# Two of eight weight units per chunk, not three, multiplied as plain f32 in the conv input projection

## The reference

```python
def _conv_mixer(h, w_in, b_in, dw_w, dw_b, ln_g, ln_b, w_out, b_out):
    u = h @ w_in + b_in                     # 256 x 2048 by 2048 x 4096
    a, gt = jnp.split(u, 2, axis=-1)
    u = a * jax.nn.sigmoid(gt)              # the gated product
    u = lax.conv_general_dilated(           # 31 taps, each channel by itself
        u, dw_w[:, None, :].astype(u.dtype), window_strides=(1,),
        padding=[(CONV_WIDTH - 1, 0)],
        dimension_numbers=('NWC', 'WIO', 'NWC'),
        feature_group_count=D_MODEL) + dw_b
    u = jax.nn.silu(_layer_norm(u, ln_g, ln_b))
    return u @ w_out + b_out
```

## Time and profile before

| | us |
|---|---|
| median of 3 runs | 2627.55 |
| lowest, highest | 2624.93, 2643.36 |
| the profiled execution | 2643.36 |
| its span, first to last instruction | 2641.7 |
| TensorE busy | 2566.5 (97%) |
| VectorE busy | 1866.8 (71%) |
| ScalarE busy | 1289.4 (49%) |
| GpSimd busy | 235.7 (9%) |
| `conv_in`, first to last matmul of its units | 1572.3 to 1791.0 |

### The profile page before, as it was taken

How to read it: one execution, slowest core, us unless ns; L and a number is a source line. 1 busy time by engine, 2 the same in 40 slices (tenths; PEclk the granted TensorE clock), 3 DMA queues, 4 the chain that set the end, 5 groups by cost and what they waited for, 6 DMA issues and landing times.

```text
span 2641.7 us, 38949 instructions
## 1 busy us (share of the span) xinstructions
PE 2566.5 (97%) x14482; PEld 2194.0 (83%) x14482; DVE 1866.8 (71%) x2076; ACT 1289.4 (49%) x1682; POOL 235.7 (9%) x270
## 2 busy tenths in 40 slices
PE   8999999999999999999999989998989999999999
PEld 7888888787877887888888878997878888888887
DVE  6796658778878766877678756988566555565565
ACT  5645445544434546454455456676544344343443
POOL 2000000010010000000000004873000000000000
PEclk9999999999999999999999989998989999999999
DMA  6644437898999765768877744453545665656655
GB/s 208 175 129 118 130 113 270 291 335 304 316 331 325 243 225 171 270 209 282 264 241 252 251 140 154 147 167 110 185 144 192 194 187 191 191 185 195 188 188 168
DMA packets 291488, 553.13 MB, mean 209 GB/s; under 512 B 17121, under 2 KB 96018, under 8 KB 290578
## 3 DMA queue, kind: packets, MB, share of 16 engines
q1 hardware_dynamic: 270994, 442.06, 51.6%
q0 software_dynamic: 18720, 102.77, 11.6%
q10 hardware_dynamic: 1632, 6.29, 0.7%
HBM read 548.96 MB, written 2.10 MB: 209 GB/s over the span
## 4 chain that ended last, share of the span: by engine, by line
PE 79%; DVE 7%; DMA 7%; issue 3%; ACT 3%; SPq 0%; POOLq 0%; DVEq 0%; ACTq 0%
PE sums L668 30%; PE small L668 10%; PE sums L697 9%; PE small L697 9%; PE sums L699 5%; DMA mod_raw<-in_mod_w_dram 5%; PE small L699 4%; PE sums L716 4%; DVE w_lo L622 2%; PE sums L718 2%; DVE mod_acc L1333 2%; ACT w_hi L613 1%; PE small L1696 1%; DMA raw<-in_w_br_dn_dram 1%; PE sums L1833 0%
## 5 line engine op out<-in xcount | busy, mean ns | idle before, releaser
L613 ACT ACTIVATE w_hi<-raw 128x1024 fp32r<-128x1024 f32 x814 | 860.5, 1060 | 1208.5 <-PE sums L668 344.3
L622 DVE TENSOR_TENSOR w_lo<-raw,w_hi 128x1024 fp32r<-128x1024 f32 x814 | 1004.2, 1242 | 617.4 <-ACT w_hi L613 615.2
L697 PE MATMUL sums<-x_two,w_hi 128*128 128x512 f32 x1024 | 367.3, 403 | 5.1 <-DVE x_two L977 2.8
L697 PE MATMUL small<-x_two,w_hi 128*128 128x512 f32 x1024 | 362.5, 399 | 0.0
L699 PE MATMUL sums<-x_two,w_lo 128*128 128x256 f32 x1024 | 289.6, 283 | 0.0
L699 PE MATMUL small<-x_two,w_lo 128*128 128x256 f32 x1024 | 287.6, 281 | 0.0
L668 PE MATMUL sums<-w_hi,x_two 128*128 128x512 f32 x896 | 283.3, 394 | 2.1 <-DVE w_lo L622 2.1
L668 PE MATMUL sums<-w_hi,y_hi 128*128 128x512 f32 x672 | 265.2, 395 | 12.7 <-issue 7.0
L668 PE MATMUL sums<-w_lo,y_hi 128*128 128x512 f32 x672 | 263.2, 392 | 0.0
L668 PE MATMUL sums<-w_hi,y_lo 128*128 128x512 f32 x672 | 263.1, 392 | 0.0
L1333 DVE SCALAR_TENSOR_TENSOR mod_acc<-mod_raw,cond,mod_acc 128x1536 f32<-128x1536 f32 x120 | 217.8, 1815 | 55.9 <-DMA mod_raw<-in_mod_w_dram 55.6
(11 more groups left out here) (412 smaller groups left out, 3953.5 us busy)
## 6 DMA issues: line engine op xcount, KB each, us to landing
raw<-in_mlp_w_dram SPq DMA_DIRECT2D x256, 512.0 KB, 4.3
raw<-in_w_in_dram SPq DMA_DIRECT2D x198, 512.0 KB, 4.7
mod_raw<-in_mod_w_dram POOLq DMA_DIRECT2D x128, 768.0 KB, 6.5
raw<-in_w_up_dram SPq DMA_DIRECT2D x128, 512.0 KB, 3.9
raw<-in_w_down_dram SPq DMA_DIRECT2D x64, 512.0 KB, 4.5
raw<-in_conv_w_in_dram SPq DMA_DIRECT2D x128, 256.0 KB, 3.7
raw<-in_w_o_dram SPq DMA_DIRECT2D x32, 512.0 KB, 6.5
raw<-in_conv_w_out_dram SPq DMA_DIRECT2D x32, 512.0 KB, 4.2
```

Source lines behind the costliest of these rows:

```text
L613: act.activation(w_hi[:, s.slot(k), :], raw[:, s.slot(k), :], ACT.Copy).then_inc(hi_ready, 1)
L622: dve.tensor_tensor(w_lo[:, s.slot(k), :], raw[:, s.slot(k), :], w_hi[:, s.slot(k), :].bitcast(F32), ALU.subtract).then_inc(lo_ready, 1)
L697: pe.matmul(to[:, b, :], w_hi[:, s.slot(k), c], both, start=kt == 0, stop=False, skip_group_check=True)
```

## The change

```diff
 CV_C = 8
 CV_B = KT // CV_C
-CV_WHOLE = (0, 3, 6)
+CV_WHOLE = (0, 4)
 POOL_TAPS = 13
```

## The result

The changed kernel takes 2645.48 us in the median of 7 runs (2634.10 to 2649.46), the kernel before 2627.55 us in the median of 7 (2624.93 to 2643.36). The ratio is 1.0056, 95% interval 1.0033 to 1.0079. A second comparison of the same two kernels gave 1.0029 (1.0012 to 1.0046). So the change makes the kernel a little slower, by 0.3 to 0.6%, where 0.2% (5.6 us) was forecast. Two profiled executions of the kernel before have spans of 2641.7 and 2627.9 us, two of the changed kernel 2634.4 and 2641.4 us: a single span can't show a difference of this size. The stage inside them can, because it repeats within 0.7 us.

The account below looks back on a forecast made before the run. In `conv_in` TensorE and VectorE were taken as nearly level, with VectorE setting the pace afterwards. -0.6, +0.6, +7.85 and -2.3 us gave +5.6, so 2633 us from the median of 2627.55, range 2621 to 2643.

Parts of the forecast that it names:

- TensorE's saving: `conv_in`: one whole unit fewer in 8 chunks saves 8 x 0.57 = 4.5 us; the four-pass sum of 7.7 was rejected.
- VectorE's cycle: `conv_in`: a sixth `w_lo` at 1.6 us lengthens the cycle from 25.99 to 27.8 us, against TensorE's 25.9.
- The two small adds: VectorE in `conv_in`: they fall in the first of the five cycles once and lie in the wait behind the gated product.
- The last chunk: Last cycle of `conv_in`: ScalarE's `tap_diag` are done in time, so 24.6 us becomes 22.3, a gain of 2.3.
- The first part: Start of `conv_in`: chunk 1's gated product 0.6 us earlier, then the 30.4 us to chunk 2 about 0.6 longer.
- the front's 3.1 us: Front of `conv_in`: added roundings for x and unit 3, costed at nothing under unit 0 at half clock, else 3.1 us.
- Where TensorE waits: TensorE in `conv_in`: waits for `w_lo` at units 5 to 7 from chunk 3 on, 1.9 us a chunk.
- The lock: `w_lo` waiting for a whole GpSimd add (1.84 us) would take 3.1 us, total 2642; ruled out by the longest, 2.25.
- TensorE as the bound: Rival for `conv_in`: VectorE keeps up, the 4.5 us and TensorE's 2.1 us of waits go, 2621 us; chance 0.12.
- the two cancel: Rival for `conv_in`: VectorE at its lower bound, 2628 us; chance 0.15.
- The clock rival: Rival for `conv_in`: TensorE's new waits lower its granted clock, 7.5 us in all, 2641 us; chance 0.07.
- The rival of late loads: Rival for `conv_in`: loads behind slot 0 late, wait behind the gated product 1 us longer in eight chunks, 2641; chance 0.06.

Follow-up runs that it names:

- the quiet pair: GpSimd's adds cut from 256 to 8 positions, in the changed kernel and in the kernel before; ratios 0.9978 and 0.9986 to the kernel before.
- quiet_pool: The changed kernel with GpSimd's adds cut from 256 to 8 positions; ratio 0.9978 to the kernel before.
- whole_0: The changed kernel with only unit 0 whole, all others split; ratio 1.0054 to the kernel before.
- early_hi: The changed kernel with `w_hi` of unit 5 written ahead of the products that wait for the gated product; ratio 1.0013 to the kernel before.
- early_hi_pool14: As early_hi, with one tap of chunks 0 to 6 moved from VectorE to ScalarE and GpSimd; ratio 1.0034 to the kernel before.

## Why the prediction was right

The forecast was 2633 us, +5.6; its mechanism, that VectorE's queue becomes the bound and its cycle is the sum of its instructions plus the wait behind the gated product, is what the runs show. The times lie above it: 1.0056 and 1.0029 of 2627.55 are 2642.3 and 2635.2 us, the first near the end of the range of 2643, and the first median itself, 2645.5, beyond it. That the second ratio comes so near to 2633 is luck in part: its interval is 9 us wide. The stage's own time is the better witness. By the steps:

- **TensorE's saving**, 4.5 us: 12.09 us from unit 0 to unit 4 is the sum to 0.01 us, the cycles of the quiet pair are 0.57 us apart, and to the last gated product the pair differs by 4.3. The prediction's sum of 7.7 us is refuted, but not the four passes (the Trainium skill, FP8 and Floating Point Precision, TensorE Precision Notes). The 16 matmuls of a whole unit start 0.216 us apart; 16 of them are the 3.45 us, and 32 passes in 3.45 us are 0.108 us each, 259 clocks of 2.4 GHz for 256 columns. The trace agrees with four passes. What the sum had wrong is a pass at 0.12 us, which is the distance of two float32r matmuls. Nor does the first split unit take 0.18 us more: it is the last f32 matmul that ends behind the start of the next row (1688.48 and 1688.51).
- **VectorE's cycle**, 27.8 us: 28.07. The wait behind the gated product was put at 1.9 and is 1.72. An added `w_lo` was taken at 1.6; the six take 10.8 us, 1.80 in the mean, against 8.25 for five. That is the term that was too small, by 0.3 us a cycle; a new pause of 0.15 us between the gated product and the taps, and the shorter wait, cancel but for 0.05. It isn't that a full queue makes every `w_lo` dearer: each costs what the add beside it leaves. Five cycles took 140.7 us, 139.0 were forecast (before: 131.15, and 132.1 in the second trace).
- **The two small adds** were put into the wait of the first of these cycles. They fall in the second, and are not quite hidden: it is 28.42 us, 0.35 over its neighbours.
- **The last chunk** gains 2.6 us, where 2.3 was forecast, because `tap_diag` is written in time: ScalarE is idle 1.79 us between the last of it and the gated product, and VectorE's wait is 1.72 us, no longer 4.55. The kernel before scatters here by 0.7 (24.58 and 23.92 us).
- **The first part**: 31.2 us for chunk 1, +0.8 where +0.6 was forecast. The stage's start to the first gated product is 35.8 us against 37.3, but 36.4 in the second trace of before; it hangs on how long unit 0 runs at 1.2 GHz: the granted clock is 0.50 for 6.1 us from the first matmul in the first trace of before and for 4.2 us in the second and in that of the changed kernel. Half of the 1.9 us between them is the 0.9 us between the two traces. Against the second -0.6 is right, the front's 3.1 us show no cost, and the stage's difference to the join is 6.9 us.
- **Where TensorE waits**: at units 5, 6 and 7, 2.16 us a chunk, 1.9 was forecast; the first two waits, 0.54 us each, come in chunk 2 already.
- **The lock**: the prediction priced the exclusive lock of the Trainium skill (SBUF — State Buffer, Who interferes with whom) at a whole add of 1.84 us and ruled it out, as no `w_lo` took 3.1. The rows show that lock. The 1.84 was a mean over seven adds of which one, of 4.41 us, had waited for three `w_lo`; an undisturbed add takes 1.26, and a `w_lo` waits only for what is left of it.
- **The sum**, +5.6 us: by the units' end 5.0 and 5.7 against the two traces of before, by the last gated product 6.3 and 6.9. What the range left out is the scatter of medians: 7 runs against 7 gave an interval 12 us wide here, and the comparison of the kernel with itself one of 10 us.

Of the rivals, TensorE as the bound (0.12) is what quiet_pool makes true, and it needs 3.5 us of contention away. That the two cancel (0.15), with `w_lo` near 1.23, falls with the six at 1.80. The clock rival falls for the change. In the windows of the changed kernel (busy PE, PEld, DVE, ACT, POOL, granted clock, DMA share, GB/s) the cycle with its three waits has a clock of 1.00:

```profile
1702.25:1730.31 28.06, 26.67 (x185) 24.87 (x184) 26.10 (x46) 17.37 (x37) 20.70 (x14) 1.00 0.47 151
```

That row shows the balance as well: VectorE is busy 26.10 of 28.06 us. But the rival was near. In whole_0 a wait of TensorE is followed by a fall to 1.2 GHz within the stage:

```profile
1633.05 0.50 PE L668 MATMUL sums<-x_two,w_hi 128*128 128x256 f32 x2 [2.58 <-DVE w_lo L622]
...
1633.45:1636.86 3.41, 3.41 (x18) 3.41 (x18) 3.41 (x5) 3.41 (x7) 3.12 (x3) 0.50 0.50 154
```

It happens once more there, behind a wait of 3.50 us, and once each in early_hi and early_hi_pool14, behind one of 2.09. The longest wait in the stage of the changed kernel is 1.46 us, and the clock stays at 1.00. Even where it fell the gated products didn't come later: the two cycles of whole_0 are 29.31 and 29.69 us, and 29.69 is the one with the two small adds. TensorE, which waits 4 us a chunk there, loses waiting time instead: behind the fall the chunk has one wait of 0.54 us left, where later chunks have three. The rival of late loads falls for the change (VectorE waits for `w_hi` behind ScalarE's products, whose `w_hi` of unit 5 has no wait noted), but a late load is what early_hi meets in chunk 1. One small sign was wrong: ScalarE was to have no waits for loads at steady pace, and has one of 0.3 to 1.9 us in four of the cycles. The one of 1.9 is for unit 3 of the next chunk; VectorE reads that `w_hi` 4.6 us later, and it costs nothing.

## What to carry to other kernels

Before work is moved from the bound engine to a second one, lay out one full cycle of the second between two marks that repeat, work and waits, and compare it with the bound's cycle: here 23.7 of 26.5 us were taken, and 1.9 us of the rest was a wait for an answer from a third engine that no shift of work removes. An engine's share of the whole span (71%) says nothing of that. Price the added instruction by what runs beside it where it will stand: here the sixth `w_lo` came among GpSimd's adds, the mean of the six was 1.80 us, and a seventh behind the last add took 1.21. And look for the cheap reorder first: an early `w_hi` on an idle ScalarE was worth as much as the whole change cost.

## What the runs showed of the hardware

A subtraction of two SBUF tensors on VectorE (128 x 1024, `w_lo`) takes 1.21 to 1.23 us with GpSimd quiet and up to 2.35 us beside GpSimd's adds; an add of GpSimd (128 x 512) 1.26 us at least and 4.47 at most. Whichever has begun goes on, and the other waits for the whole of what is left: `w_lo` lasts the rest of the running add plus 1.08 us, and at the add of 4.46 us three `w_lo` in a row ran at full pace, 3.48 us together. The taps, with one input in PSUM, stay at 0.47 to 0.49 us in either case. That agrees with the Trainium skill (SBUF — State Buffer, Who interferes with whom), which names two-input instructions from SBUF and not those with one. A wait removed is not won in full when the instruction behind it then starts at another point of GpSimd's add: early_hi gave back 0.5 of 1.72 us, its `w_lo` meeting an add with 0.70 us left and not 0.19.
